# The fronts of the RWKV units laid beside the backs of the units before them, and four attention units in flight, in a two-layer hybrid diffusion step

## The chip, the cores and the metric

One Trainium2 chip, one of its cores. The program is a single launch that runs on five engines with queues of their own: PE (matrix products and transposes into PSUM banks), DVE (elementwise work and reductions), ACT (activations and copies), POOL (elementwise work out of SBUF, and gathers), SP (issues the weight loads). They are ordered by semaphores alone; each takes its instructions in program order. All arithmetic is float32. The metric is device time in microseconds; the time before is the median of three runs.

## The reference, cut to what matters

The step runs two layers over 384 tokens: 128 context tokens and 256 latent ones, three tiles of 128. Each layer is a mixer, then a mixture of experts. Layer 0 mixes by grouped-query attention (8 heads) and by a bidirectional RWKV-7 recurrence (8 heads of 64); layer 1 by a gated DeltaNet and by differential attention. Touched here are the two attentions and the recurrence.

```python
def rwkv7_scan(S0, r, w, k, v, a, b):
    def step(S, inp):
        r_t, w_t, k_t, v_t, a_t, b_t = inp
        sa = jnp.einsum('bhij,bhj->bhi', S, a_t)
        S = S * w_t[:, :, None, :] + sa[..., None] * b_t[:, :, None, :] + v_t[..., None] * k_t[:, :, None, :]
        return S, jnp.einsum('bhij,bhj->bhi', S, r_t)
...
    for d in range(2):
        w_log = -jax.nn.softplus(-(p['b_w0'][d] + jnp.tanh(wd) @ p['b_w2'][d])) - 0.5
        a = jax.nn.sigmoid(p['b_a0'][d] + ad @ p['b_a2'][d])
        k_d = kb * (1 + (a - 1) * p['b_ka'])
        seqs = (r_h, heads(jnp.exp(-jnp.exp(w_log))), heads(k_d), v_h, -kk, kk * heads(a))
        if d == 1:
            seqs = tuple(jnp.flip(t, axis=1) for t in seqs)
        y_d, S_d = rwkv7_scan(S0[:, d], *seqs)
```

The context tokens start from a zero state and their final states are an output; the latent tokens start from a given one and run over two tiles.

## The kernel before, in words

The phases of a layer follow each other on PE, ACT and DVE, with a meeting of the three at each phase's end (`phase_end`, L280): modulation, norm, projection, attention (`attend`), the recurrence (`rwkv`, in layer 1 `delta`), output projection, router, experts.

**Weights.** All weights come in pieces of up to 1 MB through a ring of six slots (`RING`, L56). Piece n goes to slot n modulo 6; SP waits in `wait_slot_free` (L300) until the piece six before it has been used. Layer 1's modulation weights (six rows of four quarters, 24 pieces) are used during the RWKV phase of layer 0, one row for each unit; behind them come the four pieces of the output projection, three of the shared expert, and the routed experts.

**Attention** (PE L711, ACT L1381, DVE L1783). 24 units, one for each tile of queries and head; the first eight see one tile of keys, the other sixteen three. A unit is `scores` (L724) into one of two banks, a maximum on DVE, an exponential on ACT into one of two buffers, transposes of the weights on PE (`turn`, L735; the transposes have line L741 in the trace), a copy on ACT, and the weighted sum of the values (`weigh`, L745). In one round PE does the scores of unit u, the transposes of u-1 and the weighted sum of u-2.

**RWKV** (PE L809, ACT L1425, DVE L1854). Six units (`RWKV_UNITS`, L346), each a tile and a direction: (0, forward), (0, backward), (1, forward), (2, backward), (2, forward), (1, backward). The first two begin from a zero state, the others read a state (`from_state`, L801); the first four keep a new state (`RWKV_KEEPS`, L348). The recurrence over 128 tokens is turned into matrices: products of decayed keys with each other (grams), the inverse of a triangular matrix, and products with the values. A unit has a front and a back.

- Front: two low-rank ("lora") products for decay and gate; their biases on DVE; two sigmoids on ACT, each of three steps; running decay sums on PE; exponentials on ACT; the keys scaled on DVE; sixteen transposes (trace line L839); copies on ACT (L1448, L1449) and DVE; gram products, which DVE masks into `r_nr` and `r_ak`. Between these, PE does the unit's row of the modulation (`mod_rows_part`, L608) and the turning of the previous row (`turn_mods`, L622).
- Back: the read of the state and of the values; the inverse of eight 64x64 blocks at a time, doubled in five levels (`invert`, PE L772: products, a copy by ACT L1418, joins, an addition by DVE in `join`, L1837), for which POOL masks the off-diagonal parts (`masked_parts`, L2296, trace line L2311); the solution of the first half of the tokens, its effect on the second half, the solution of the second; output and new state.

All buffers of a unit but those of the inverse exist once, and a unit's first products wait for `unit_saved` of the unit before. So front and back of one unit, and then the next unit, follow each other. After the last unit DVE normalises and gates the result.

Nearly all matrix products have line L596 in the trace (the helper `mm`), DVE's operations L1628 (`tt`), L1636 (`stt`) and L1642 (`copy`), ACT's activations L1261 (`f`).

## Time and profile before

| | |
|---|---|
| time, median of 3 runs | 2732.3 us (2722.39 to 2732.45) |
| the profiled execution | 2728.02 us, of which its span 2726.4 us |
| PE busy | 2162.3 us (79% of the span) |
| PE weight loads busy | 1484.6 us (54%) |
| DVE, ACT, POOL busy | 803.8, 370.0, 322.5 us |
| mean granted PE clock | 0.867 |
| chain that ended last | PE 54%, DMA 26%, DVE 11% |

How to read it: a granted clock of 1.0 is 2.4 GHz and 0.5 is 1.2 GHz, and the chip grants one of the two at a time; a mean between them is a mixture. Busy times of PE are modelled at their ends, so a busy PE is not PE at its best. "Idle before" in square brackets is the idle time of that engine ahead of a row, with what ended it. Times within the span are counted from its start. Attention of layer 0 lies at 223 to 292 us, RWKV at 303 to 685, its normalisation to 708, attention of layer 1 at 1681 to 1750.

### The profile page before, as it was taken

To read this page: it belongs to the slowest core of one execution; us is meant where nothing else is said; L and a number is where in the kernel's file an instruction comes from. 1 tells how busy PE (TensorE), PEld (TensorE's weight loads), DVE (VectorE), ACT (ScalarE), POOL (GpSimd) and SP (SyncE) were. 2 spreads that over 40 slices of the span, in tenths; PEclk is the share of its full clock that TensorE was granted. 3 is DMA by queue.
4 is the path that set the end of the run, shared out by engine and by line. 5 is a ranking of instruction groups with operands and counts; after the bars stand their busy time and mean duration, and the time that the engine had idled before them with its cause. 6 is when DMAs were issued, how large, how long until landed. Compare 5 with 4: busy or idle time off the path is not lost.

```text
span 2726.4 us, 37243 instructions
## 1 busy us (share of the span) xinstructions
PE 2162.3 (79%) x15513; PEld 1484.6 (54%) x15513; DVE 803.8 (29%) x1628; ACT 370.0 (14%) x827; POOL 322.5 (12%) x380
## 2 busy tenths in 40 slices
PE   5998788888488888988973998677488888888882
PEld 2445566667375555655541445466475655555551
DVE  1132433333432111111115261455623111111114
ACT  0002222112011111111110022211101111111110
POOL 0000222222000111111110000022200111111110
PEclk8995787777688999999996997578788999999996
DMA  7542111111123999999993212000012899999994
GB/s 300 200 171 65 63 63 63 67 63 63 51 85 132 404 397 387 402 409 404 394 365 133 93 47 101 0 1 9 1 66 76 327 410 404 401 398 399 396 380 189
DMA packets 122401, 571.20 MB, mean 210 GB/s; under 512 B 26352, under 2 KB 30064, under 8 KB 70768
## 3 DMA queue, kind: packets, MB, share of 16 engines
q1 hardware_dynamic: 85392, 496.07, 46.3%
q0 software_dynamic: 26624, 56.67, 5.5%
q10 hardware_dynamic: 10208, 15.95, 1.7%
q8 instruction: 128, 2.10, 0.3%
q14 instruction: 49, 0.40, 0.0%
HBM read 564.36 MB, written 46.20 MB: 224 GB/s over the span
## 4 chain that ended last, share of the span: by engine, by line
PE 54%; DMA 26%; DVE 11%; issue 3%; ACT 1%; ACTq 1%; PEld 1%; SPq 1%; POOL 1%; PEldq 0%; DVEq 0%; POOLq 0%
PE bank L596 50%; DMA ring<-in_exp_w_up 13%; DVE arena L1628 6%; DMA ring<-in_exp_w_down 6%; DMA ring<-in_exp_w_gate 3%; DMA mixed<-choice_rows 2%; PE bank L741 1%; ACTq L1273 1%; PEld bank L596 1%; PE bank L1161 1%; DVE mixed L1628 1%; ACT arena L1261 1%; PE bank L839 1%; DVE hT L1633 1%; SPq L324 1%
## 5 line engine op out<-in xcount | busy, mean ns | idle before, releaser
L596 PE MATMUL bank<-ring,arena 128*64 128x256 f32 (+3 forms) x5168 | 876.5, 434 | 150.9 <-DMA ring<-in_exp_w_up 62.1
L596 PEld LDWEIGHTS bank<-ring,arena 128*64 128x64 f32 (+1 forms) x5168 | 528.9, 150 | 446.4 <-issue 352.9
L596 PE MATMUL bank<-arena 64*64 64x64 f32 (+9 forms) x6260 | 448.8, 258 | 55.3 <-DVE arena L1628 33.3
L596 PEld LDWEIGHTS bank<-arena 64*64 64x64 f32 (+3 forms) x6260 | 389.9, 165 | 96.9 <-issue 52.3
L1642 DVE COPY arena<-bank 128x512 f32<-128x512 f32 (+3 forms) x291 | 153.4, 532 | 861.3 <-PE bank L596 464.9
L596 PE MATMUL bank<-ring,hT 128*128 128x512 f32 (+2 forms) x672 | 266.6, 554 | 20.3 <-DVE hT L1633 18.2
L2311 POOL TENSOR_TENSOR arena<-arena,consts 64x256 f32<-64x256 f32 x216 | 161.3, 747 | 1013.3 <-DVE arena L1628 559.6
L596 PEld LDWEIGHTS bank<-ring,hT 128*128 128x128 f32 x672 | 127.0, 197 | 159.6 <-issue 138.5
L2325 POOL DMA_INDIRECT choice_rows<-arena x76 | 76.6, 1008 | 703.6 <-DVE arena L1642 703.6
L2319 POOL DMA_INDIRECT arena<-token_rows,arena x76 | 78.0, 1026 | 633.6 <-DVE arena L1632 603.0
L596 PE MATMUL bank<-hT,ring 128*128 128x384 f32 x384 | 128.3, 495 | 21.7 <-ACT hT L1508 20.9
L1636 DVE SCALAR_TENSOR_TENSOR arena<-bank,arena 128x256 f32<-128x256 f32 (+2 forms) x90 | 45.0, 500 | 337.6 <-PE bank L596 337.2
L596 PEld LDWEIGHTS bank<-hT,ring 128*128 128x128 f32 x384 | 104.8, 275 | 41.5 <-ACT hT L1508 21.1
L596 PE MATMUL bank<-arena,consts 128*128 128x512 f32 (+3 forms) x228 | 95.7, 562 | 31.2 <-ACT arena L1261 16.2
L1628 DVE TENSOR_TENSOR arena<-arena 128x512 f32<-128x512 f32 (+7 forms) x135 | 105.9, 800 | 45.8 <-DMA arena<-choice_rows 34.6
L1564 ACT COPY arena<-bank 128x256 f32<-128x256 f32 x76 | 28.4, 373 | 669.9 <-PE bank L1188 669.9
L1628 DVE TENSOR_TENSOR arena<-arena,bank 128x256 f32<-128x256 f32 (+2 forms) x196 | 81.3, 448 | 112.5 <-PE bank L596 112.0
L596 PEld LDWEIGHTS bank<-arena,consts 128*128 128x128 f32 x228 | 44.0, 214 | 81.5 <-issue 70.5
L1161 PE MATMUL bank<-consts,arena 128*128 128x128 f32 x608 | 80.6, 277 | 9.5 <-issue 9.5
L1570 ACT COPY arena<-bank 128x512 f32<-128x512 f32 x76 | 44.6, 586 | 281.8 <-PE bank L596 281.8
L596 PE MATMUL bank<-ring,cond 128*32 128x512 f32 x384 | 60.7, 761 | 24.8 <-DMA rope<-in_rope 19.3
L1161 PEld LDWEIGHTS bank<-consts,arena 128*128 128x128 f32 x608 | 70.9, 144 | 11.3 <-issue 11.1
(155 smaller groups left out, 1293.5 us busy)
## 6 DMA issues: line engine op xcount, KB each, us to landing
ring<-in_exp_w_gate SPq DMA_DIRECT2D x128, 1024.0 KB, 10.2
ring<-in_exp_w_up SPq DMA_DIRECT2D x128, 1024.0 KB, 11.5
ring<-in_exp_w_down SPq DMA_DIRECT2D x128, 1024.0 KB, 11.8
ring<-in_mod_w SPq DMA_DIRECT2D x48, 1024.0 KB, 7.3
ring<-in_od_w_in SPq DMA_DIRECT2D x14, 1024.0 KB, 7.3
arena<-choice_rows POOLq DMA_DIRECT2D x4, 3072.0 KB, 14.2
ring<-in_ev_w_in SPq DMA_DIRECT2D x10, 1024.0 KB, 10.4
ring<-in_ev_w_out SPq DMA_DIRECT2D x4, 1024.0 KB, 6.5
```

The source lines that it names most:

```text
L324: sp.dma_start(slot(n).rearrange("p (c k) -> p c k", c=c), src[l, bass.ds(expert[r], 1)].rearrange("e (p c) n -> (e p) c n", c=c))\
L596: return nc.tensor.matmul(out, lhsT, rhs, start=start, stop=stop, **kw)
L741: last = nc.tensor.transpose(bank[2 + u % 2][:, k * P:(k + 1) * P], A.p[:, u % 2, k * P:(k + 1) * P], C["ident"])
L1161: last = nc.tensor.transpose(bank[c // 4][:, (c % 4) * P:(c % 4 + 1) * P], g_x[u % 2][:, c * P:(c + 1) * P], C["ident"])
L1564: nc.scalar.copy(g_ht[u % 2], heads(bank[4][:, 0:2 * P], 2)).then_inc(sem("ht_saved"), 1)
L1570: nc.scalar.copy(g_y[u % 2][:, 0:512], bank[5][:, :]).then_inc(sem("slots_saved"), 1)
L1628: return nc.vector.tensor_tensor(out, a, b, op)
L1636: return nc.vector.scalar_tensor_tensor(out=out, in0=a, scalar=s, in1=b, op0=op0, op1=op1)
L1642: return nc.vector.tensor_copy(out, a)
L2311: last = nc.gpsimd.tensor_tensor(inv.off[k % 2][g][p, :, :], inv.nt[g][p, :, p], mask, ALU.mult)
L2319: nc.gpsimd.indirect_dma_start(g_x[u % 2], None, x_rows[l], rows, bounds_check=NTOK - 1, oob_is_err=False).then_inc(sem("gathered", u % 2) ...
L2325: nc.gpsimd.indirect_dma_start(y_rows[l], rows, g_y[u % 2], None, bounds_check=TOP_K * NTOK - 1, oob_is_err=False).then_inc(sem("scattered ...
```

## The change

Attention: four units in flight. Scores go to banks 0, 1, 6 and 7 in turn (`DEPTH`, `score_banks`), the exponentials to four buffers; in one round PE does the scores of u, the transposes of u-3 and the weighted sum of u-4.

RWKV: what survives a unit's front (`r_ar`, `r_nr`, `r_ak`, the two key tiles, `r_sw`, `r_ec`) exists twice, and the front of unit u+1 is written, step by step, between the levels of unit u's inverse and its last products. The second set lies in ring slots 0 to 2, which are lent from the first piece of layer 1's modulation to the end of RWKV; in that time the pieces go through slots 3 to 5 alone (`ring_places`), and the piece that first returns to slot 0, the last of the output projection, waits for all six units. The banks of the inverse are rearranged: both gram products now use banks 0 to 3, one after the other, and the inverse banks 4 to 7. The gates and the last modulation row move from behind the last unit to its inverse. The arithmetic of layer 1's `delta` stays as it was.

```diff
+SHARED = 3
...
+            a, b = at["mod", 1, 0, 0], at["out", 0]
+            lent = [i for i in range(a, a + RING) if i % RING >= SHARED]
+            order = [i % RING for i in lent] + list(range(SHARED))
...
+                if n < a:
+                    at_slot[n] = n % RING
+                elif n < b:
+                    at_slot[n] = lent[(n - a) % len(lent)] % RING
+                else:
+                    at_slot[n] = order[(n - b) % RING]
...
-            m = n - RING
+            m = piece_before[n]
+            if m is None:
+                return
+            if n == returned:
+                sp.wait_ge(sem("unit_saved"), len(RWKV_UNITS))
...
+        DEPTH = 4
+        score_banks = (0, 1, 6, 7)
...
+        r_ar = [pairs_of(r_ar0), pairs_of(ring[:, 2, 0:1024])]
...
+        r_nr = [[pairs_of(a) for a in (r_nr0, r_nr1)], [pairs_of(ring[:, 0, 1024 * g:1024 * (g + 1)]) for g in range(2)]]
+        r_ak = [[pairs_of(a) for a in (r_ak0, r_ak1)], [pairs_of(ring[:, 1, 1024 * g:1024 * (g + 1)]) for g in range(2)]]
...
-                for u in range(26):
+                for u in range(24 + DEPTH):
                     if u < 24:
                         scores(u)
-                    if 1 <= u <= 24:
-                        turn(u - 1)
-                    if u >= 2:
-                        weigh(u - 2)
+                    if DEPTH - 1 <= u < 24 + DEPTH - 1:
+                        turn(u - DEPTH + 1)
+                    if u >= DEPTH:
+                        weigh(u - DEPTH)
...
+            def unit_mods(u, quarters):
+                pe.wait_ge(sem("zw_sum"), u + 1)
+                mod_rows_part(1, u, 1, quarters)
+
+            def decay_sums(u):
+                t, d = RWKV_UNITS[u]
+                pe.wait_ge(sem("zw_sum"), u + 1)
+                if u:
+                    turn_mods(1, u - 1, 0, 2 * J, next_rows)
+                pe.wait_ge(sem("sig_ready"), 2 * u + 1)
+                mm(bank[2][:, :], C[f"cum_incl{d}"], r_sig)
+                mm(bank[3][:, :], C[f"cum_excl{d}"], r_sig)
...
+            def grams(u, n):
+                if n == 0:
+                    pe.wait_ge(sem("arT_saved"), u + 1)
+                    pe.wait_ge(sem("bkT_saved"), u + 1)
+                else:
+                    for g in range(2):
+                        pe.wait_ge(r_inverse[0].sem("nt_ready", g), u + 1)
...
+                lora_products(0)
+                unit_mods(0, (0, 1))
+                decay_sums(0)
+                unit_mods(0, (2, 3))
+                turn_unit(0)
+                grams(0, 0)
+                grams(0, 1)
...
+                    if u:
+                        pe.wait_ge(sem("unit_saved"), u)
+                    turn_blocks(inv, u)
+                    if t:
+                        from_state(u, 0)
+                    pe.wait_ge(sem("gram_saved"), 2 * u + 2)
...
+                    if more:
+                        lora_products(u + 1)
+                    level_products(inv, u, 1)
+                    if more:
+                        unit_mods(u + 1, (0,))
+                    else:
+                        turn_mods(1, u, 0, 2 * J, next_rows)
+                        for k in range(TILES):
+                            last = mm(bank[1 + k][:, :], gt_of(k), r_g2)
+                        last.then_inc(sem("gate_ready"), 1)
                     pe.wait_ge(sem("read_saved"), u + 1)
+                    level_joins(inv, u, 1)
+                    level_products(inv, u, 2)
+                    if more:
+                        decay_sums(u + 1)
+                    level_joins(inv, u, 2)
+                    level_products(inv, u, 3)
+                    if more:
+                        unit_mods(u + 1, (1,))
+                    level_joins(inv, u, 3)
+                    level_products(inv, u, 4)
+                    if more:
+                        unit_mods(u + 1, (2,))
+                    level_joins(inv, u, 4)
+                    if more:
+                        unit_mods(u + 1, (3,))
+                    level_products(inv, u, 5)
+                    level_joins(inv, u, 5)
+                    if more:
+                        turn_unit(u + 1)
...
+                    if more:
+                        grams(u + 1, 0)
...
                     last.then_inc(sem("y_unit_ready"), 1)
...
+                    if more:
+                        grams(u + 1, 1)
...
+                    save_products(inv, u, 1)
+                    if more:
+                        write_rate(u + 1)
+                    save_products(inv, u, 2)
+                    if more:
+                        gate_sigmoid(u + 1)
+                    save_products(inv, u, 3)
+                    if more:
+                        decay_exps(u + 1)
+                    save_products(inv, u, 4)
+                    save_products(inv, u, 5)
+                    if more:
+                        save_next_mods(u)
+                        save_next_rows(u + 1).then_inc(sem("mod_rows_saved"), 1)
+                        save_turned(u + 1)
...
+                    open_blocks(inv, u)
+                    if more:
+                        rate_inputs(u + 1)
+                    add_joins(inv, u, 1)
+                    add_joins(inv, u, 2)
+                    if more:
+                        gated_keys(u + 1)
+                    add_joins(inv, u, 3)
+                    add_joins(inv, u, 4)
+                    if more:
+                        decayed(u + 1)
+                    add_joins(inv, u, 5)
+                    if more:
+                        save_keys(u + 1)
...
+                    if more:
+                        mask_grams(u + 1, 0)
                     dve.wait_ge(sem("y_unit_ready"), u + 1)
...
                     last.then_inc(sem("unit_saved"), 1)
                     dve.wait_ge(sem("unit_saved"), u + 1)
+                    if more:
+                        mask_grams(u + 1, 1)
```

The new functions hold the steps of the old loop body: on PE `lora_products`, `unit_mods`, `decay_sums`, `turn_unit`, `grams`; on ACT `write_rate`, `gate_sigmoid` (the two sigmoids), `decay_exps`, `save_turned`; on DVE `rate_inputs` (the two biases), `gated_keys`, `decayed`, `save_keys`, `mask_grams`. `turn_blocks`, `level_products`, `level_joins`, `save_products`, `open_blocks` and `add_joins` are the old `invert` and `join`, cut by level.

## Rows read from the trace of the kernel before

**Rows 1.** Busy us by stretch, each engine (instructions); then PE clock, DMA share, GB/s.

```profile
237.00:291.00 54.00, 54.00 (x171) 36.35 (x170) 9.97 (x19) 16.24 (x47) 0.00 (x0) 0.50 0.00 0
1698.00:1746.00 48.00, 48.00 (x146) 31.08 (x145) 13.24 (x34) 13.53 (x39) 0.00 (x0) 0.50 0.00 1
302.80:685.30 382.50, 315.53 (x4448) 257.21 (x4448) 146.01 (x288) 78.84 (x181) 104.98 (x144) 0.80 0.19 68
...
517.00:527.50 10.50, 9.02 (x98) 8.79 (x100) 3.79 (x7) 1.02 (x3) 5.69 (x9) 0.52 0.00 0
527.50:548.00 20.50, 19.03 (x485) 17.44 (x482) 7.68 (x20) 4.82 (x13) 9.85 (x14) 0.99 0.02 4
548.00:559.30 11.30, 8.68 (x64) 8.41 (x65) 2.34 (x6) 0.00 (x0) 0.00 (x0) 0.51 0.00 0
...
685.00:708.00 23.00, 6.93 (x38) 3.86 (x38) 22.52 (x16) 0.60 (x3) 0.00 (x0) 0.57 0.00 0
```

**Rows 2.** Timeline, an attention unit: start, us, engine, line, operation [idle before].

```profile
255.67 0.58 ACT L1261 ACTIVATE arena<-bank,arena 128x384 f32<-128x384 f32 x1 [2.54 <-DVE arena L1639]
...
258.55 0.90 PE L741 MATMUL bank<-consts,arena 128*128 128x128 f32 x3
```

**Rows 3.** Timeline, two levels of the inverse of RWKV unit 3, PE.

```profile
530.57 3.23 PE L596 MATMUL bank<-arena 64*64 64x64 f32 x96 [0.25 <-DVE arena L1628]
...
534.05 3.23 PE L596 MATMUL bank<-arena 64*64 64x64 f32 x96 [0.25 <-DVE arena L1628]
```

**Rows 4.** Timeline, RWKV fronts: transposes of unit 0, unit 3, start of 4.

```profile
317.30 1.97 PE L839 MATMUL bank<-consts,arena 128*128 128x128 f32 x16 [2.48 <-DVE arena L1628]
...
492.71 2.09 PE L596 MATMUL bank<-consts,params 128*64 128x2 f32 x32
...
498.22 0.69 DVE L1636 SCALAR_TENSOR_TENSOR arena<-arena 128x512 f32<-128x512 f32 x1 [4.04 <-ACT arena L1261]
498.30 3.02 PE L596 MATMUL bank<-arena,consts 128*128 128x512 f32 x4
...
502.04 1.92 PE L596 MATMUL bank<-ring,cond 128*32 128x512 f32 x16
502.14 1.57 ACT L1261 ACTIVATE arena<-bank 128x512 f32<-128x512 f32 x3 [3.96 <-PE bank L596]
...
504.23 2.49 DVE L1628 TENSOR_TENSOR arena<-arena 128x512 f32<-128x512 f32 x4
...
506.78 3.27 PE L839 MATMUL bank<-consts,arena 128*128 128x128 f32 x16 [2.82 <-DVE arena L1628]
...
511.51 3.72 PE L596 MATMUL bank<-arena 64*128 64x256 f32 x32 [1.47 <-DVE arena L1642]
...
559.30 2.08 PE L596 MATMUL bank<-hT,arena 64*128 64x512 f32 x4 [2.62 <-DVE params L1628]
```

**Rows 5.** Timeline, RWKV backs, PE: read of unit 0, then pieces of unit 3.

```profile
327.70 2.00 PE L596 MATMUL bank<-arena 128*128 128x64 f32 x16 [3.24 <-DVE arena L1628]
...
520.38 3.67 PE L596 MATMUL bank<-arena 128*128 128x64 f32 x16
...
523.99 1.97 PE L596 MATMUL bank<-consts,arena 64*64 64x64 f32 x32
...
546.88 1.11 PE L596 MATMUL bank<-params,arena 64*128 64x64 f32 x16 [0.46 <-ACT arena L1459]
...
547.92 8.76 PE L596 MATMUL bank<-arena 128*128 128x64 f32 x64
```

**Rows 6.** Groups by line and shape, RWKV: busy us, mean ns, idle before.

```profile
L2311 POOL TENSOR_TENSOR arena<-arena,consts 64x256 f32<-64x256 f32 x144 | 105.0, 729 | 562.5 <-DVE arena L1628 553.8
...
L1628 DVE TENSOR_TENSOR arena<-arena,consts 128x256 f32<-128x256 f32 x12 | 9.6, 838 | 0.0
...
L1628 DVE TENSOR_TENSOR params<-params 128x256 f32<-128x256 f32 x4 | 1.7, 425 | 12.9 <-ACT params L1261 12.9
```

**Rows 7.** The page's DMA issues: operation, count, KB each, median us to landing.

```profile
ring<-in_mod_w SPq DMA_DIRECT2D x48, 1024.0 KB, 7.3
```

More of the change, by code:

```diff
@@ L268, in build, with ring_places @@
         loops = [at["experts", l] for l in range(LAYERS)]
+        RWKV_UNITS = [(0, 0), (0, 1), (1, 0), (2, 1), (2, 0), (1, 1)]
+        def ring_places():
+            a, b = at["mod", 1, 0, 0], at["out", 0]
+            lent = [i for i in range(a, a + RING) if i % RING >= SHARED]
+            order = [i % RING for i in lent] + list(range(SHARED))
+            at_slot, turn = {}, 0
+            for n in range(len(pieces)):
+                if n < a:
[4 more added lines that the diff above has]
+                    at_slot[n] = order[(n - b) % RING]
+            last, before, count, held = {}, {}, {}, {}
+            for n in range(len(pieces)):
+                s = at_slot[n]
+                before[n] = last.get(s)
+                last[s] = n
+                held[s] = held.get(s, 0) + 1
+                count[n] = held[s]
+            return at_slot, before, count
+        slot_of, piece_before, piece_count = ring_places()
+        returned = at["out", 0] + [slot_of[at["out", 0] + i] for i in range(RING)].index(0)
         def slot(n):
-            return ring[:, n % RING, :]
+            return ring[:, slot_of[n], :]
         def piece_value(n):
-            return 16 * (n // RING + 1)
+            return 16 * piece_count[n]
         block = ctx.enter_context(nc.Block())
@@ L407, in build, with __init__ @@
         class Inverse:
-            def __init__(self, nt, off, t, tt, m1):
+            def __init__(self, nt, off, t, tt, m1, at=None):
+                at = at or {"m": (4, 0), "turned": (4, 1), "t": (6, 0), "tt": (6, 1)}
+                self.out = [{k: bank[b + g][:, 256 * i:256 * (i + 1)].rearrange("p (h n) -> p h n", h=4)
+                             for k, (b, i) in at.items()} for g in range(2)]
                 four = lambda aps: [a.rearrange("p (h n) -> p h n", h=4) if len(a.shape) == 2 else a for a in aps]
@@ new lines, in unit_mods @@
+            def unit_mods(u, quarters):
+                pe.wait_ge(sem("zw_sum"), u + 1)
+                mod_rows_part(1, u, 1, quarters)
+            def decay_sums(u):
+                t, d = RWKV_UNITS[u]
+                pe.wait_ge(sem("zw_sum"), u + 1)
[4 more added lines that the diff above has]
+                mm(bank[3][:, :], C[f"cum_excl{d}"], r_sig)
+                for j in range(4):
+                    last = mm(bank[0][:, 2 * j:2 * j + 2], r_sig[:, 128 * j:128 * (j + 1)], halves)
+                last.then_inc(sem("cum_ready"), 1)
@@ L1392, in attend @@
                         .then_inc(sem("qT_saved"), 1)
-                for u in range(25):
+                for u in range(24 + DEPTH - 1):
                     if u < 24:
@@ new lines, in add_joins, with rate_inputs @@
+            def add_joins(inv, n, k):
+                for g in range(2):
+                    dve.wait_ge(inv.sem("join_ready", g), (LEVELS - 1) * n + k)
+                    dve.wait_ge(inv.sem("t_ready", g), LEVELS * n + k)
+                    if k < LEVELS - 1:
+                        tt(inv.t[g], inv.t[g], inv.out[g]["t"], ALU.add)
+                    tt(inv.tt[g], inv.tt[g], inv.out[g]["tt"], ALU.add).then_inc(inv.sem("t_ready", g), 1)
+            def rate_inputs(u):
+                t, d = RWKV_UNITS[u]
+                dve.wait_ge(sem("za_ready"), u + 1)
+                tt(r_sig, bank[0][:, :], r_w0[:, 512 * d:512 * (d + 1)], ALU.add)
+                tt(r_gate, bank[1][:, :], r_a0[:, 512 * d:512 * (d + 1)], ALU.add).then_inc(sem("zw_sum"), 1)
@@ new lines, in save_keys, with mask_grams @@
+            def save_keys(u):
+                dve.wait_ge(sem("tokT_ready"), u + 1)
+                copy(r_bt, heads(bank[2][:, :], 4))
+                copy(r_kt, heads(bank[3][:, :], 4)).then_inc(sem("bkT_saved"), 1)
+            def mask_grams(u, n):
+                t, d = RWKV_UNITS[u]
+                mask = masks[d].unsqueeze(1).broadcast_to([P, 2, 256])
+                dst = (r_nr, r_ak)[n][u % 2]
+                dve.wait_ge(sem("gram_ready"), 2 * u + n + 1)
+                for g in range(2):
+                    for i in range(2):
+                        last = tt(dst[g][:, 2 * i:2 * i + 2, :, :].rearrange("p c k n -> p c (k n)"),
+                                  heads(bank[2 * g + i][:, :], 2), mask, ALU.mult)
+                    last.then_inc(r_inverse[0].sem("nt_ready", g) if n == 0 else sem("gram_saved"), 1)
```

339 lines of the change are left out of this document (165 added, 174 removed).

## The prediction

> **What bounds the kernel now.** I began with the page's engine table, where PE is far ahead of every other engine, and went on to the busy times by stage [rows 1], which show where a change of this kind can earn. In both attention stretches PE is busy for every microsecond, at a granted clock of 0.50 (1.2 GHz). In the RWKV stretch, 382.5 us for six units, PE is busy 315.5 us at a mean clock of 0.80: 67 us idle, and much of the rest at the lower level.
>
> Next, the timeline of one attention unit [rows 2]: the softmax exponential of a unit starts at 255.67 and takes 0.58, but the transposes that wait for it start at 258.55, over 2 us after it has ended. PE reaches them late; it does not wait for them. So the period of about 3.6 us is PE's own work.
>
> Last, RWKV unit 3 (unit 4 for its first product). In the front PE alternates between short bursts and waits for ACT and DVE [rows 4]: 2.82 us before the transposes, 1.47 before the gram products, 3.24 before the first read [rows 5]. Inside the inverse this is not so: a level repeats every 3.48 us [rows 3], with a hand-off idle of about 0.25, so PE has next to no room there. The clock follows the bursts: about 0.5 from 517 to 527.5, after the waits around the gram masks, about 1.0 through the inverse, 0.51 again in the output products [rows 1].
>
> So RWKV is bound by PE's work plus its waits in the fronts, attention by PE alone. These stages follow each other, with the weights of the experts loaded behind them, so what RWKV saves the end saves.
>
> **The change part by part.** *Attention.* Four score tiles in place of two; scores, transposes and weighted sums are the same in number and order of kinds. Nothing that PE waited for is removed, since it waited for nothing. What is left is the ramp at the start, where PE waits for the first exponentials: I take 1 us for both layers, bounds 0 and 2.
>
> *RWKV, one unit in the steady state.* The front of the next unit is cut in pieces and put into the back of this one, so a period now holds all PE work of a unit, and I sum PE's path from one end of output products to the next, at the 2.4 GHz level first:
> - DVE's results (at most five operations of 0.42 [rows 6]) must be saved before the next unit's inverse begins; the second half of the gram products (half of 3.72 [rows 4], 1.9) runs beneath: 2.4 with hand-offs.
> - Turning the blocks 1.97, state product 1.11, read 2.00 [rows 5]: 5.1. The mask of the second grams (four operations of the shape of which DVE does four in 2.49 [rows 4]) lies beneath the first two.
> - The lora products of the unit after: 2.08 at 0.50 [rows 4], no row at full clock; between 1.04 and 2.08. I take 1.04 here and put the rest into the clock term. PE then waits 0.3 for DVE's two sums (half of those 2.49, 1.25), which lie mostly beneath the level's products.
> - Inverse: four levels of 3.48 [rows 3] and a last one without a third of its products (64 at 3.23/96, and a hand-off), 2.4: 16.3.
> - Inserted: four quarters of the modulation product, 1.92/2 each, 3.8; turned modulation 2.09; decay sums (from 498.30 to the next products at 502.04, 3.7 at low clock) 2.7: 8.6 [rows 4]. They were not free in the front either; here they fill at most the 0.25 per level.
> - Wait for the decayed keys 0.5, the drain behind the last quarter 0.4, sixteen transposes 1.97 [rows 4] and 0.1: 3.0.
> - The two half solves. First solve, sixteen products at 1.97/32 [rows 5], 1.0; then ACT, which first has two copies of the transposes to make (three operations of that shape take 1.57 [rows 4]), so 0.8 of wait; cross products 0.6, first gram half 1.9, second solve 0.7, estimates by the same rate: 5.0.
> - State product 1.1, output 32 products at 2.00/16 [rows 5] 4.0, new state (what 8.76 at low clock leaves beside 32 products at 3.67/16 is 1.4, half of the 4.0 is 2.0) 2.0: 7.1.
>
> Together 48.8. To this I add 1.0 for hand-offs (0.25 to 0.46 each [rows 3, 5]) and two terms with bounds.
>
> *DVE beside POOL.* DVE's key and decay operations (three of 0.69, 2.0, and 2.49 with 0.42, 2.9 [rows 4, 6]) move from the front, where POOL is idle, to the inverse, where POOL masks. Of one shape, 128x256 out of SBUF, DVE needs 0.838 beside POOL's masks and 0.425 elsewhere [rows 6]. Doubling what coincides (the three key operations beside the masks of the last level) costs 2 us of DVE, of which the joins wait for about 1: I take 1.0, bounds 0 and 5. The Trainium skill (SBUF — State Buffer, section "SBUF: two separate sides") says that VectorE with two SBUF inputs and GpSimd share a port pair by an exclusive lock, the loser blocking for the whole instruction; the doubled row agrees, and by the rule seven operations that each wait out a mask (0.73 [rows 6]) would be 5.1 per unit, and the time 2706.
>
> *Clock.* Price of the low level, per unit: output products 3.67/16 against 2.00/16, 32 of them: 3.3; gram halves, no row, between 0 and 1.9 each; state products, no row at this level, up to 1.1, taken 0.9; read 1.67; lora 1.04; transposes 1.3 [rows 4, 5]. If the low level lasts from the output to the lora, as it does in the trace, it costs about 8.8; with transposes and the other grams, 12; none if the denser stream holds the clock. I take 5, bounds 0 and 12, because the new stream has gram and lora products where the old one had waits.
>
> Full unit: 55.8. By unit:
> - Unit 0: its front still runs alone. Loop start to read was 327.7 - 302.8 = 24.9. The gram halves now share banks, so the second waits for the first mask: +2.5. The ring keeps three slots, so the fourth quarter is loaded only when the first is used; bounds 0 and the 7.3 of a landing [rows 7], taken 3. 30.4, then a unit without what lies ahead of the read (2.4 and 1.97) and without state products (2.2): 49.2. 79.6.
> - Unit 1, no state products: 53.6. Units 2 and 3: 55.8 each. Unit 4, no new state: 53.8.
> - Unit 5 without a front (18 less, 4.7 more for the gate and the last turned modulation, 1 less for POOL) 41.5, and 0.9 for its results: 42.4.
>
> Sum 341.0 against 382.5: 41.5 less, with attention 42.5.
>
> *Ring.* In the steady state the fourth quarter needs the slot of the first, used some 19 us before; a landing takes 7.3 [rows 7], so it hides, with 12 us to spare. SP now waits, before the last piece of the output weights, for all six units, and behind that stand the two shared pieces: three loads that lie beneath DVE's normalisation, 22.5 us of the 23 after the units [rows 1]; were that cover gone, about 7. POOL's masks (four of 0.73 per level, 2.9) keep ahead of levels of 3.48, for the levels only become longer.
>
> **The rivals.**
> - *The clock holds.* Every price of the low level falls away: 6 units by 5, about 30 less. For it: gram and lora products stand where waits stood. Against: the output products and solves, before which the clock falls in the trace, stay. 2655. Chance 0.16.
> - *The clock stays as low as now* and the hand-offs reach their upper row: 7 + 2 more per unit, about 40 more. For it: the output stretch at 0.51 is long [rows 1], and the turned modulation, whose products are two columns wide, now splits the inverse. 2722, no change. Chance 0.12.
> - *The other side: waits in line.* ACT and DVE take their work in order, and the front's pieces now stand ahead of the copies and adds that each level needs: ACT 4.0 for both gates (DVE waits 4.04 for them [rows 4]) and 1.6 for the exponentials, DVE 1.25, 2.0 and 2.9: 12 per unit. Wholly exposed in five units it is 60, and the kernel is 18 slower: 2746. It decides from 8.5 of the 12: then the gain is gone. Against: PE has an inserted piece of its own nearly each time. Chance 0.06.
> - *The inverse itself falls to 1.2 GHz*, split by narrow products: a level of 3.23 busy at most doubles, 15 per unit, 2760 at worst. Against: the levels stay at 0.99 [rows 1] and are dense. Chance 0.03.
> - *The change does what it says in attention too*: the clock rises there, and then four in flight is what sustains it; PE's scores and transposes would halve, about 1.4 of 3.6 in 32 long units, 45 less: 2640. Against: PE was wholly busy there and stayed at 0.50 in both layers, and its stream is the same. Chance 0.04.
>
> **How the numbers follow.** The profiled execution took 2728.0 us; the median of the runs is 2732.3, their lowest 2722.4, so the trace stands for them within 0.2%. 2728.0 - 42.5 = 2685.5; I give 2686. Chance of the forecast itself, with its bounds for clock, POOL and hand-offs (2665 to 2710): 0.59. The range reaches from the holding clock to nearly no gain: 2654 to 2718. This kernel's measurement tells 0.5%, 13.7 us, from no change: faster by more 0.83 (forecast, holding clock, attention and a little of the second rival), same 0.10, slower 0.07.
>
> **What would show it.** Right: PE idle in RWKV falls from 67 us to about 30, the six units take about 341; the attention stretches keep their length and 0.50; levels are longer than 3.48 only by the inserted pieces; the two-input operations of DVE beside POOL's masks take over 0.8. Wrong: attention shorter by more than 3 us (the clock rose); joins waiting for ACT or DVE for more than 1 us at several levels (the rival of waits in line); PE waiting for modulation weights in units after the first (the ring); a mean clock in RWKV below 0.75 or above 0.9 (the clock term).

## The result, and the profile after

The changed kernel took 2647.6 us as the median of four runs (2626.25, 2639.20, 2655.95, 2659.22), against 2727.4 for the kernel before beside it: a ratio of 0.970, 95% interval 0.963 to 0.978. The forecast was 2686, with a range of 2654 to 2718. The direction was right, the gain was nearly twice as large as forecast (80 us against 42), and the median lies 6 us below the range.

The page of the changed kernel: engines with their busy us, share of the span and instructions, then the shares of the chain that ended last. The profiled execution is the shortest of the four, 2626.25 us, and its span is 2624.5.

```profile
PE 2102.2 (80%) x15513; PEld 1433.7 (55%) x15513; DVE 799.4 (30%) x1626; ACT 367.2 (14%) x827; POOL 326.4 (12%) x380
...
PE 55%; DMA 26%; DVE 10%; issue 3%; ACT 1%; ACTq 1%; PEld 1%; SPq 1%; POOL 1%; PEldq 0%; DVEq 0%; POOLq 0%
```

The same work needs 60 us less of PE's busy time. PE's instructions are as many as before, so they ran faster; the granted clock rose from 0.867 to 0.892. Busy times by stretch, with the columns of [rows 1]: RWKV as a whole; its six units, each to the end of its output and new state; layer 0's attention; two pieces of layer 1's attention.

```profile
295.40:604.50 309.10, 284.45 (x4486) 224.46 (x4486) 142.45 (x286) 76.64 (x181) 110.03 (x144) 0.91 0.24 84
...
295.40:370.80 75.40, 63.24 (x818) 45.18 (x818) 34.67 (x60) 20.27 (x45) 22.59 (x30) 0.84 0.32 113
370.80:419.30 48.50, 45.34 (x740) 35.59 (x738) 23.46 (x48) 12.69 (x30) 18.56 (x25) 0.93 0.25 89
419.30:467.70 48.40, 46.09 (x773) 36.70 (x770) 23.55 (x48) 12.58 (x30) 19.51 (x26) 0.96 0.27 94
467.70:515.90 48.20, 45.83 (x770) 36.65 (x768) 23.88 (x49) 12.69 (x30) 18.50 (x25) 0.96 0.26 89
515.90:561.60 45.70, 43.46 (x742) 35.12 (x738) 23.90 (x49) 12.58 (x30) 17.60 (x24) 1.00 0.27 94
561.60:604.50 42.90, 40.50 (x663) 35.24 (x662) 12.99 (x32) 5.83 (x16) 13.27 (x19) 0.82 0.01 2
...
217.00:285.00 68.00, 67.56 (x216) 46.59 (x216) 12.85 (x28) 22.10 (x73) 0.00 (x0) 0.50 0.04 13
...
1602.00:1628.40 26.40, 26.34 (x71) 15.44 (x71) 8.18 (x22) 9.25 (x37) 0.00 (x0) 0.50 0.01 2
1630.60:1650.40 19.80, 19.55 (x119) 13.94 (x119) 9.59 (x24) 10.22 (x29) 0.00 (x0) 1.00 0.00 1
```

RWKV went from 382.5 [rows 1] to 309.1. PE's idle time there fell from 67.0 to 24.6, its busy time from 315.5 to 284.5, and the clock rose from 0.80 to 0.91. In layer 1's attention the clock rose to 1.00 at about 1630 and stayed; in the trace before both attentions lie wholly at 0.50 [rows 1]. From the first of a unit's transposes to the last, that stretch was 66.9 us long before and 48.3 after; layer 0's, 64.5 and 62.7. A last 5.5 us lie ahead of all this: layer 0's first such transpose comes at 219.41 instead of 224.95, and a second trace of the same kernel (below) has it at 224.76, so this is variation of the start. The account for the profiled run: 2728.0 - 73.4 - 20.4 - 5.5 = 2628.7, against 2626.25.

PE's timeline in unit 2 of the changed kernel (start, us, what; idle before in brackets), from the lora products of unit 3 to the second half of its grams:

```profile
425.87 1.13 PE L634 MATMUL bank<-hT,arena 64*128 64x512 f32 x4
...
433.03 2.09 PE L634 MATMUL bank<-consts,params 128*64 128x2 f32 x32
435.05 3.68 PE L634 MATMUL bank<-params,consts 128*128 128x512 f32 x4
...
444.08 3.71 PE L634 MATMUL bank<-arena 64*64 64x64 f32 x96
...
457.78 1.14 PE L634 MATMUL bank<-arena 64*64 64x64 f32 x16 [0.35 <-ACT arena L1585]
458.85 2.00 PE L634 MATMUL bank<-ring,arena 64*128 64x256 f32 x16
460.78 1.14 PE L634 MATMUL bank<-arena 64*64 64x64 f32 x16
461.85 1.11 PE L634 MATMUL bank<-params,arena 64*128 64x64 f32 x16
462.89 4.87 PE L634 MATMUL bank<-arena 128*128 128x64 f32 x64
467.69 2.00 PE L634 MATMUL bank<-ring,arena 64*128 64x256 f32 x16
```

The 64 products of output and new state, 8.76 before [rows 5], take 4.87: they run at the full clock, with the gram products between the half solves. The lora products take 1.13 instead of 2.08 [rows 4]. Only the decay sums behind the two-column products of the turned modulation are slow: 3.68. In unit 4, where the clock never fell, they take 1.99.

### The profile page after: what moved, and what is told of

It reads as the page before. It is cut to its first block, busy times and chain, and to the rows that moved or that the text cites. A ratio compares the mean times of both kernels' runs of the same rounds, so it can differ in the third digit from the quotient of the medians.

```text
span 2624.5 us, 37277 instructions
## 1 busy us (share of the span) xinstructions
PE 2102.2 (80%) x15513; PEld 1433.7 (55%) x15513; DVE 799.4 (30%) x1626; ACT 367.2 (14%) x827; POOL 326.4 (12%) x380
## 4 chain that ended last, share of the span: by engine, by line
PE 55%; DMA 26%; DVE 10%; issue 3%; ACT 1%; ACTq 1%; PEld 1%; SPq 1%; POOL 1%; PEldq 0%; DVEq 0%; POOLq 0%
PE bank L634 51%; DMA ring<-in_exp_w_up 17%; DVE arena L1755 5%; DMA ring<-in_exp_w_down 4%; DMA mixed<-choice_rows 2%; DMA ring<-in_exp_w_gate 2%; ACTq L1373 1%; PEld bank L634 1%; PE bank L1261 1%; PE bank L779 1%; DVE mixed L1755 1%; DVE hT L1760 1%; SPq L356 1%; DVE xT L1763 1%; DVE stats L1766 1%
## 5 line engine op out<-in xcount | busy, mean ns | idle before, releaser
L634 PE MATMUL bank<-ring,arena 128*64 128x256 f32 (+4 forms) x5264 | 889.1, 433 | 148.1 <-DMA ring<-in_exp_w_up 58.6
L634 PEld LDWEIGHTS bank<-ring,arena 128*64 128x64 f32 (+2 forms) x5264 | 535.7, 150 | 447.1 <-issue 354.6
L634 PE MATMUL bank<-arena 64*64 64x64 f32 (+8 forms) x5972 | 376.9, 243 | 45.4 <-DVE arena L1755 29.2
L634 PEld LDWEIGHTS bank<-arena 64*64 64x64 f32 (+3 forms) x5972 | 321.3, 153 | 107.3 <-issue 76.2
L2484 POOL TENSOR_TENSOR arena<-arena,consts 64x256 f32<-64x256 f32 x144 | 111.2, 772 | 822.2 <-DVE arena L1769 420.6
L1755 DVE TENSOR_TENSOR arena<-arena,bank 128x256 f32<-128x256 f32 (+3 forms) x198 | 81.8, 447 | 136.1 <-PE bank L634 134.2
L634 PE MATMUL bank<-arena,consts 128*128 128x512 f32 (+3 forms) x204 | 81.9, 546 | 28.1 <-ACT arena L1361 13.2
L1755 DVE TENSOR_TENSOR arena<-arena 128x512 f32<-128x512 f32 (+7 forms) x111 | 90.5, 821 | 42.7 <-DMA arena<-choice_rows 35.4
L1261 PE MATMUL bank<-consts,arena 128*128 128x128 f32 x608 | 80.6, 277 | 9.2 <-issue 9.2
L1333 PE MATMUL bank<-consts,arena 128*128 128x128 f32 x48 | 10.5, 412 | 82.8 <-DVEq L2443 82.8
L634 PE MATMUL bank<-ring,cond 128*32 128x512 f32 x384 | 53.0, 654 | 28.3 <-DMA rope<-in_rope 19.5
```

The source lines that it names most:

```text
L634: return nc.tensor.matmul(out, lhsT, rhs, start=start, stop=stop, **kw)
L1261: last = nc.tensor.transpose(bank[c // 4][:, (c % 4) * P:(c % 4 + 1) * P], g_x[u % 2][:, c * P:(c + 1) * P], C["ident"])
L1755: return nc.vector.tensor_tensor(out, a, b, op)
L2484: last = nc.gpsimd.tensor_tensor(inv.off[k % 2][g][p, :, :], inv.nt[g][p, :, p], mask, ALU.mult)
```

## The experiments

Theory: the waits in the fronts cost twice, once as waits and once because the clock falls after them, and the change removes both; four attention units in flight do little by themselves, and the clock in layer 1's attention is not the change's doing. Rivals: depth raises the attention's clock; RWKV's gain is overlap alone; the new banks and buffers help by themselves.

**Two units in flight** in the changed kernel.

```diff
-        DEPTH = 4
-        score_banks = (0, 1, 6, 7)
+        DEPTH = 2
+        score_banks = (0, 1)
```

> The changed kernel with attention back to two units in flight, so that only the RWKV half of the change is left. My theory: the six RWKV units keep their 305 us (PE idle about 23 us), both attentions run wholly at a granted clock of 0.50 and take 67 to 68 us each, as in the kernel before; the profiled run of the change had 48.3 us in layer 1's attention, so this one comes to about 2645 us. Rival (depth has no part in the clock of layer 1's attention): the clock rises there with two in flight as well, and the stretch falls below 60 us, the time below 2640.

**Four units in flight** in the kernel before: the attention half of the diff alone.

> The kernel before with four attention units in flight and nothing else. My theory: PE waited for nothing in attention, so both attentions keep 66 to 68 us at 0.50 and the time stays at 2727, within 6 us. Rival (four in flight is what lets the clock rise): layer 1's attention falls to about 48 us and the time to about 2708; if layer 0's rises too, to about 2690.

**The changed kernel again.**

> The changed kernel once more, for a second profile. If the RWKV stretch owes its 305 us to the order of the work, it is 303 to 308 again. If layer 1's attention rose to the full clock by the moment at which the rise fell in one run, its length differs: 48 where it rises at about the 19th unit before its end, 67 where it does not; the time moves with it, between 2626 and 2660.

Measured: 2659.9 us for two in flight (ratio 0.974, 0.971 to 0.978); 2722.1 for four in flight in the kernel before (0.998, 0.996 to 1.000); 2644.2 for the changed kernel again (2635.7 to 2655.1). Windows with the columns as above, RWKV and then layer 1's attention, of the run with two in flight:

```profile
302.60:616.30 313.70, 288.30 (x4486) 226.98 (x4486) 142.86 (x286) 76.61 (x181) 109.89 (x144) 0.90 0.24 83
1613.50:1680.50 67.00, 67.00 (x200) 43.49 (x201) 18.15 (x47) 20.66 (x69) 0.00 (x0) 0.50 0.01 2
```

and of the changed kernel again:

```profile
300.80:616.60 315.80, 290.80 (x4486) 229.74 (x4486) 142.93 (x286) 76.61 (x181) 109.73 (x144) 0.89 0.24 83
1613.80:1677.50 63.70, 63.67 (x196) 41.08 (x197) 17.77 (x46) 20.58 (x69) 0.00 (x0) 0.51 0.01 2
```

RWKV keeps its gain without the attention's half, and is 309 to 316 long in these three traces; I had expected 303 to 308, and 2645 us for two in flight. The clock's rise in layer 1 does not come in every execution of the changed kernel: its second trace has none before the last units. Four in flight save 1.8 us in layer 0 (62.7 against 64.5) and 3.3 in layer 1 at the low clock.

By the medians they save more: 12 to 16 us in the changed kernel (2647.6 and 2644.2 against 2659.9), 4 in the kernel before (2722.1 against 2726.4). The four runs with two in flight lie within 1.1 us. The eight with four reach from 2626 to 2659: five lie under 2650, at a granted clock of 0.887 to 0.892 over the whole execution, the other three at 0.879 to 0.882, like those with two. So the shorter runs are those with more clock; that the clock rose in attention is shown only for the one of the five that has a trace. A rise late in attention with two in flight is on record too, in the trace of the filled kernel below. Whether four in flight make an early rise likelier is not settled, and that rival stands.

**Both gram products behind the unit's output.**

```diff
-                    if more:
-                        grams(u + 1, 0)
...
                     if more:
+                        grams(u + 1, 0)
                         grams(u + 1, 1)
```

DVE's masks move with them.

> The changed kernel with both gram products of the next unit put behind the unit's output, instead of one between the half solves and one behind the output. Theory A (the gram products in the waits of the solves hold the clock for the output): the solves and the output products go back to about 0.5, which costs 3.3 for the output, up to 2 for the new state and about 1 for the solves and state products, 5 to 6 in each of five units, beside about 3.5 of exposed waits: RWKV about 350 us, the time about 45 over the change. Theory B (the clock is held by something else, such as the absence of the waits in the front): only the waits come back, RWKV about 322 us, the time about 17 over the change.

Measured: 2674.1 us, 30 over the changed kernel beside it. RWKV as a whole:

```profile
300.40:640.50 340.10, 300.92 (x4486) 238.03 (x4486) 143.52 (x286) 76.64 (x181) 109.80 (x144) 0.87 0.22 77
```

PE's timeline, with the exposed wait for the first mask, and the output and new state of unit 2:

```profile
444.60 3.64 PE L634 MATMUL bank<-arena 64*128 64x256 f32 x16 [2.75 <-DVE arena L1754]
...
487.98 4.87 PE L634 MATMUL bank<-arena 128*128 128x64 f32 x64
```

It lies between the two theories: against the second trace PE's idle time rises by 14 (25.0 to 39.2) and its busy time by 10. In unit 1 the clock was at 0.50 from 428 to 440, over solves and output; in unit 2 it was 1.00 there (4.87). So the clock can hold through solves and output without the gram products between the solves; whether their absence lowered it in unit 1 is not shown by this one trace. Moving one product costs both kinds of time at once.

**The front in line**: the changed kernel with `lora_products` to `grams` of unit u+1, and their ACT and DVE steps, put whole behind unit u.

> The changed kernel with the front of the next unit put whole behind the unit, on PE, ACT and DVE, so that nothing overlaps; the lent ring slots, the doubled buffers, the shared gram banks and four attention units in flight stay. Theory: waits and lower clock both come back, 67 us a unit, and 2.7 per unit for the second gram products that wait for the first mask: RWKV 380 to 398, the time 2715 to 2735. Rival (the new banks and buffers help by themselves): RWKV below 365, the time below 2700.

Measured: 2728.9 us (ratio 0.999, 0.996 to 1.001).

```profile
301.30:696.60 395.30, 328.29 (x4486) 255.62 (x4486) 139.91 (x286) 78.70 (x181) 103.95 (x144) 0.78 0.19 66
```

All is given back: idle 67.0 as before, busy 328.3, the clock 0.78. Banks, buffers and ring bring nothing by themselves. In this trace, that of the slowest of ten runs (2737.4), RWKV is 13 us longer than before.

**The clock by itself.** The kernel before, not overlapped, with products that change no result put into PE's waits, first 23 a unit, then 11.

```diff
+            def fill(n, b=6):
+                for _ in range(n):
+                    mm(bank[b][:, :], C["ident"], r_w0[:, 0:512])
...
+                        fill(4)
                         pe.wait_ge(sem("unit_saved"), u)
...
+                    fill(5)
                     pe.wait_ge(sem("tok_ready"), u + 1)
```

> The kernel before with 23 extra products of 512 columns per RWKV unit put where PE waits: before the next unit's lora products, the transposes, the grams, the read and in the half solves. They go to a bank that is free and change no result. At the full clock one takes 0.38 (3.02 for four at 0.50, 1.98 for four in a mixture), 8.7 per unit against 11 of idle time per unit. Theory (the clock falls because of the waits): it then holds, the products of a unit that ran at 0.50 run at 1.0, and RWKV goes from 382 to about 355 us, the time to about 2700. Rival (the waits are not what lowers the clock): the fillers run at 0.50, 17.4 per unit against 11, RWKV about 415, the time about 2760.

> The kernel before with 11 extra products of 512 columns per RWKV unit in its waits, in place of 23. In the run with 23, one took 0.93 at the full clock (3.70 for four), not the 0.38 that I had reckoned: 21.4 per unit in about 11 of waiting, while the clock stood at 0.98 and unit 3 took 65.8 with them, so about 44 without. 11 of them are 10.2 and should lie wholly inside the waits. Theory (the lower clock costs as much as the waits do): the clock stays above 0.93, a unit of the steady state takes 55 to 57 in place of 67 to 69, RWKV about 325, the time about 2675, with nothing overlapped. Rival (the fewer products do not hold the clock): mean clock below 0.85, RWKV above 360, the time 2710 or more.

Measured: 2731.5 us with 23 (ratio 1.002, 1.001 to 1.003), 2687.7 with 11 (0.984, 0.982 to 0.986). RWKV with 23, and the end of layer 1's attention in the same trace, whose clock rose at 1744.2 with two units in flight and no product of mine near it:

```profile
302.70:695.20 392.50, 381.48 (x4716) 260.00 (x4716) 146.11 (x288) 78.79 (x181) 104.87 (x144) 0.98 0.18 66
1744.20:1753.00 8.80, 8.39 (x48) 5.60 (x47) 3.73 (x9) 4.16 (x12) 0.00 (x0) 1.00 0.00 0
```

and two rows of PE's timeline, four of the extra products and the output of unit 3 with its new state:

```profile
497.45 3.70 PE L596 MATMUL bank<-hT,consts 128*128 128x512 f32 x8
...
558.48 4.87 PE L596 MATMUL bank<-arena 128*128 128x64 f32 x64
```

RWKV with 11, and one unit of it:

```profile
299.90:649.40 349.50, 327.98 (x4576) 240.50 (x4576) 146.04 (x288) 78.79 (x182) 104.92 (x144) 0.96 0.20 75
416.90:474.90 58.00, 54.43 (x793) 40.38 (x792) 24.79 (x50) 13.06 (x30) 17.48 (x24) 1.00 0.21 79
```

My first fill was mis-sized: a product is two instructions, so four (x8) take 3.70, and 23 are twice what the waits hold. It is still the best measure of the work itself. The 134 extra products take 134 x 0.925 = 124; without them PE was busy for 257 us, at a clock of 0.98, with work for which it needs 315.5 before. So the kernel before spends its 382.5 us as 257 of work, 58 for the lower clock and 67 of waits. With 11 the extra 64 take about 60, the work 268, and RWKV is 33 us shorter with nothing overlapped: the clock alone is nearly half of what the change brings. The 325 that I expected was missed, since the fillers lengthen the waits (idle and fillers 81.5 against 67) and the clock still fell at times.

**DVE's key operations twice.**

> The changed kernel with DVE's three key operations done twice in the units after the first, to the same result: in the second run of the change they take 0.68, 1.22 and 1.10 beside POOL's masks (0.69 each without), so 3.0 more of DVE in each of five units. Theory (DVE's extra time beside POOL lies under PE's inserted pieces): at most 1 us per unit, RWKV 309 to 320. Rival (the joins wait for it, as my term of 1.0 per unit supposes): 2 to 3 per unit, RWKV 322 to 330, the time about 2657.

Measured: 2670.7 us (ratio 0.979, 0.977 to 0.980). RWKV as a whole:

```profile
301.30:629.10 327.80, 289.39 (x4486) 226.38 (x4486) 156.47 (x301) 76.65 (x181) 111.29 (x144) 0.90 0.23 80
```

and PE's timeline in unit 2, the joins behind the keys and what follows:

```profile
464.80 1.97 PE L634 MATMUL bank<-arena 64*64 64x64 f32 x32 [2.97 <-DVE arena L1755]
466.70 1.75 PE L634 MATMUL bank<-ring,cond 128*32 128x512 f32 x8
```

My theory falls. Of 3.0 more on DVE 2.97 stand in the path, and behind this wait the clock drops to 0.50 and comes back at about 468. RWKV is 12 us longer than in the second trace. The changed kernel has no wait there, but also nothing to spare: DVE's keys fill the room in the level to the end.

**Attention at the full clock.** Products of 512 columns ahead of one unit's scores, into the bank that these scores overwrite: ten ahead of the ninth unit, ten ahead of the first, ten ahead of the ninth with two in flight; then five with four in flight, six with two, and six in the kernel before.

```diff
+                    if u == 8:
+                        for _ in range(10):
+                            mm(bank[score_banks[u % DEPTH]][:, :], C["ident"], A.qt[:, 0, :, :])
```

> The changed kernel with ten products of 512 columns, 7.5 us at 1.2 GHz, in both attentions ahead of the scores of the ninth unit, the first with three tiles of keys. They go to the bank that these scores overwrite. Theory (the attention holds the full clock once it has it, and did not have it because nothing raised it): the clock rises in both layers, the sixteen long units take about 2.0 in place of 3.6 to 3.7 each, 26 us less per layer for 6 to 7 of products: about 20 less per layer, the time near 2615 and the spread of the runs small. Rival (it rises for the products alone): it falls back within some units, most of all in layer 0, whose weighted sums have half the columns; the time is 7 to 15 above the changed kernel.

> The same ten products ahead of the first unit of both attentions, so that the eight short units come first after them. Theory: if the short units hold the clock too, they take about 1.0 in place of 1.56 and the gain is 4 more per layer than with the products at the ninth unit, the time about 2607. Rival: a short unit is bound by the exponential's chain at the full clock, PE waits, the clock falls before the long units, and the products only cost 6 to 7 per layer: about 2655.

> As with the products at the ninth unit, but with two attention units in flight. Theory (four in flight is needed at the full clock, since from the scores of a unit to its transposes lie about 2 us of maximum and exponential, and a unit takes PE 2.0): PE waits in each unit, a unit takes 2.3 to 2.6, and either the clock falls again or about 10 to 14 less per layer is left than with two in flight and no products (2660): 2635. Rival (depth does not matter at either clock): the same gain as with four, 2620.

> The changed kernel with five products of 512 columns ahead of the ninth attention unit in both layers, in place of ten. The ten took 11.49 in layer 0, of which the clock was at 0.50 for the first 5.4. Theory (what raises the clock is the first half of them): the rise comes as before, and the second half, 4.5 to 5 per layer, is saved: about 2612 as median, lowest about 2602. Rival (five are too few in some runs): the runs split, some at 2605 and some at 2655.

> The changed kernel with two attention units in flight and six products of 512 columns ahead of the ninth unit, in place of ten. With four in flight and five products the clock rose in layer 1 and fell again after PE had waited 0.60 for ACT's copy, so the runs split. Theory (with two in flight less is queued on ACT and DVE when PE comes from the products, so PE does not wait and the clock stays): the clock holds in both layers to their end in every run, 4 products fewer save 4 per layer, the median about 2617, the runs within 10 us of each other. Rival (the rise depends on the number of products, not on the depth): six are too few, the runs split between 2615 and 2660.

> The kernel before with the same six products ahead of the ninth attention unit in both layers, and nothing else. Theory (what the products bring has nothing to do with the change): as with the changed kernel at two in flight, about 40 us less, 2688. Rival (it needs the new order of the work): less than 20.

| run | median us | runs | ratio to before |
|---|---|---|---|
| ten at unit 9, four in flight | 2620.7 | 2611.7 to 2646.1 | 0.964 |
| ten at unit 1, four in flight | 2665.9 | 2659.2 to 2675.0 | 0.979 |
| ten at unit 9, two in flight | 2625.0 | 2619.3 to 2626.2 | 0.962 |
| five at unit 9, four in flight | 2625.9 | 2613.8 to 2637.8 | 0.961 |
| six at unit 9, two in flight | 2616.1 | 2614.2 to 2622.9 | 0.959 (0.958 to 0.961) |
| six at unit 9, kernel before | 2689.0 | 2679.8 to 2695.1 | 0.985 (0.983 to 0.987) |

(Ten products are 11.5 us in layer 0, not 7.5, for the reason given above.) Six products, two in flight: windows of the long units in layers 0 and 1.

```profile
244.00:271.00 27.00, 27.00 (x156) 18.43 (x155) 9.41 (x18) 14.78 (x43) 0.00 (x0) 1.00 0.00 1
1614.00:1642.00 28.00, 28.00 (x157) 18.61 (x156) 13.88 (x35) 14.75 (x43) 0.00 (x0) 1.00 0.00 1
```

Five products, four in flight, layer 1: PE after the products.

```profile
1607.61 0.33 PE L782 MATMUL bank<-consts,arena 128*128 128x128 f32 x1
1608.54 2.37 PE L634 MATMUL bank<-arena 128*128 128x128 f32 x4 [0.60 <-ACT arena L1511]
```

The same stream of attention runs at 0.50 or at 1.00, wholly busy at either. Behind the products at the ninth unit it stayed at 1.00 to the end in the traces in which PE did not wait there, in layer 0 too. My theory on depth falls: with two in flight PE does not wait at the full clock either (27.00 of 27.00), and the runs lie closest together. With four in flight and five products the clock rose in layer 1 and fell again at 1608.6, behind a wait of 0.60 for ACT. With six and two in flight it held in both layers of the trace, and all five runs lie within 9 us; from this one pair it isn't settled whether depth or the sixth product decides. With ten and with five products and four in flight the runs spread over 34 and 24 us, where I had expected a small spread and 2612. Ahead of the first unit the products are lost: in the short units of layer 0 PE waits twice for 0.20, and from 236 us on the clock is 0.50 again. In the kernel before the six products bring 39 us, about as much as in the changed one with two in flight (44): this gain is no part of the change. The version with six products and two in flight is faster than both kernels.

## Why the prediction missed

**What held.** PE was bound by its work and its waits in RWKV, and at 0.50 the attention's length was mostly its own work. Four in flight changed that length by 5 us all the same, where I had 1 (bounds 0 to 2). No wait for a weight load longer than 0.3 us stands in RWKV, so the ring cost nothing. In unit 0 the fourth quarter came in time (my 3 us were not there), but I had overlooked that `unit_mods` shares bank 1 with the lora products and must wait for DVE; that wait is 3.14. The second gram half waits 2.67 (I had 2.5). Loop start to read, 30.4 forecast, was 31.6 (295.4 to 327.0). PE's timeline of the changed kernel's unit 0, modulation and second gram half:

```profile
300.76 3.64 PE L634 MATMUL bank<-ring,cond 128*32 128x512 f32 x16 [3.14 <-DVE ring L1755]
...
321.55 2.91 PE L634 MATMUL bank<-arena 64*128 64x256 f32 x16 [2.67 <-DVE arena L1755]
```

**The step that failed** is the clock term: "I take 5, bounds 0 and 12". Unit 4 ran wholly at 1.00 and took 45.7; with the new state that it lacks (4.87 less 3.79 for the 32 products of output alone, 1.1) a full unit at the full clock is 46.8. Units 2 and 3 took 48.4 and 48.2, so the clock costs them 1.5, not 5. Units 2 to 4 of the second trace:

```profile
428.10:476.45 48.35, 46.05 (x774) 36.78 (x770) 23.56 (x48) 12.58 (x30) 19.55 (x26) 0.96 0.28 94
476.45:527.35 50.90, 48.66 (x770) 39.28 (x768) 23.89 (x49) 12.69 (x30) 18.39 (x24) 0.90 0.25 85
527.35:574.50 47.15, 44.90 (x742) 35.77 (x738) 23.92 (x49) 12.58 (x30) 17.61 (x24) 0.96 0.27 91
```

There the term is 1.5, 4.1 and 1.4. Unit 5, which has no next front beside it, ran at 0.82 and took 42.9 against my 42.4, so in that unit the forecast was not too long. By stretch the forecast of 341 with about 30 idle meant 311 of PE's time, 4.5 less than before; measured were 31 less in one trace and 25 less in the other. The waits came out nearly as forecast: 42 less, against 37. The reason that I gave against a clock that holds, that the output products and solves before which it falls would stay, was wrong: it is not these products that lower the clock but what stands between them. With waits filled in the old order the same 64 products took 4.87 as well.

The rest of the unit was too long by about as much: 48.8 + 1.0 + 1.0 against 46.8. Of the 7.5 by which units 2 and 3 came out shorter than my 55.8, 3.5 are the clock term and 4.0 are this. The blocks took 1.15 at the full clock (my 1.97 was a row at 0.50, so low clock stood in the sum at the full clock too), the new state 1.1 (2.0), the transposes 1.9 with no wait (3.0). DVE beside POOL does slow down. In unit 2 of the changed kernel, DVE's three key operations and POOL's four masks:

```profile
442.24 0.68 DVE L1763 SCALAR_TENSOR_TENSOR arena<-arena,ring 128x512 f32<-128x512 f32 x1
442.85 1.22 DVE L1763 SCALAR_TENSOR_TENSOR arena<-ring,params 128x512 f32<-128x512 f32 x1
444.10 1.10 DVE L1763 SCALAR_TENSOR_TENSOR arena<-arena 128x512 f32<-128x512 f32 x1
442.30 4.27 POOL L2484 TENSOR_TENSOR arena<-arena,consts 64x256 f32<-64x256 f32 x4 [6.96 <-PE bank L634]
```

Against 0.69 in the front [rows 4] two of them are longer, 0.9 together, and the masks take 4.27 in place of four times 0.73 [rows 6]. But none of it reaches PE, so that term is 0, with no room left, as the doubled keys show.

In the trace the two engines alternate: POOL's first two masks end at 443.51 and 444.65, and DVE's two longer operations end 0.55 behind each, at 444.06 and 445.20. The Trainium skill (SBUF — State Buffer, section "SBUF: two separate sides") has the loser of the shared ports wait for the whole instruction of the other; these rows agree. What failed is my count for 2706, seven operations that each wait out a whole mask. Two waited in this unit, each for what was left of a mask, and the four decay operations met no mask in any unit.

**The rivals.** "The clock holds" (2655) is nearly what RWKV did; I gave it 0.16. Without an early rise in attention the changed kernel takes 2655 (the second trace), just within the range. What brought the profiled run below it is the clock in layer 1's attention, which I had tied to four in flight (0.04). It rose early in one of two traces of the same kernel. Why it rose at 1630 in one run and not in another with the same stream stays open, and so does whether it did so in the other runs below 2650: only two of the eight have a trace. Two of my own signs of a wrong forecast came: an attention shorter by more than 3 us (18.6, in the second trace 3.3), and a clock above 0.9 in RWKV (0.91, in the second trace 0.89). The rival of a clock that stays low has a wrong sum: 7 + 2 more in five units is 45, so 2731 and not 2722. "Waits in line" did not happen, but the doubled keys show how near it was.

The Trainium skill (TensorE: Matmul & The Clock Gate, section "HAM oscillation — how this bites in real kernels") says that a long enough wait of PE throttles the clock, and that the slow start behind it is paid for at each such wait. The clock of 0.50 behind the 2.97 of the doubled keys agrees, and so does the 0.96 to 0.98 of the filled kernels. Waits are not all that decides: attention stayed at 1.2 GHz for over 60 us with no wait of PE.

## What to carry to other kernels

Where the trace shows waits of PE followed by products at the lower clock, price both: here 67 us of waits had 58 us of slow products behind them, and one edit took back 42 and 25 to 31. Before overlapping anything, fill the waits with idle products in the old order: the clock's share is then measured nearly by itself, though the fillers lengthen the waits a little. And a stretch that is wholly busy at 1.2 GHz need not be at its limit: a few wide products ahead of it may raise the clock, and the stretch may hold it.

## What was not expected of the hardware

- One stream of products, wholly busy, has two lengths: 16 long attention units at 0.50 (3.7 us each in layer 1) or at 1.00 (1.99). In the first trace of the changed kernel it passed from one to the other at 1630 with no wait of PE nearby; in the second it did not before 1676.
- Thirty-two products of two columns (2.09 us, PE busy throughout) were followed by the lower clock in units 0 to 3 of the changed kernel (decay sums of 3.4 to 3.7), and not in unit 4 (1.99). In the second trace unit 4 has it too (3.44).
- DVE's operations on two SBUF operands and POOL's masks hold each other up in turn: two of DVE's took 1.22 and 1.10 in place of 0.69, and three of POOL's 1.21, 1.08 and 1.06 in place of 0.73.
